# A transformer pair of blocks on one core: packed S5 near coefficients, swept first units, scores ahead of turned probabilities

## The chip, the cores and the metric

One core of a Trainium2 chip. The metric is device time in microseconds of one execution; a run's time is compared as the median of several runs.

## The reference

Two blocks of two layers each on a sequence of 256 tokens, width 1024, in fp32. What the change touches, cut down:

```python
def _mixer_s5(h, ...):                 # 64 groups of 16 channels, 64 complex states each, two directions
    bu = einsum('sgc,gpc->sgp', us, b_bar[direction])
    h  = associative_scan(a, bu, reverse=(direction == 1))
    y += einsum('sgp,gcp->sgc', h_re, c_re) - einsum('sgp,gcp->sgc', h_im, c_im)
    z  = gelu(y + d_skip * u);  return (z @ w_glu_a) * sigmoid(z @ w_glu_b)

x = x + gate_f * (square(relu(h @ w_fc1)) @ w_fc2)              # the MLP after each mixer of the first block

def swa_sink_attention(q, k, v, sinks):                          # window 128, 16 heads on 4 kv heads
    scores = where(valid, q @ k.T / 8, -inf);  m = maximum(max(scores), sink)
    e = exp(scores - m);  probs = e / (sum(e) + exp(sink - m));  return probs @ v

h = h + sigmoid(rms_norm(h) @ gate_w) * (p_i @ proj_w)           # per-layer embedding, in both layers
```

## The kernel before

**Layout.** Activations lie transposed, 8 tiles of 128 channels by 256 tokens (`xT`, `hT`, `sq`). Weights come as 1 MB blocks (8 tiles of 128 rows by 256 columns) into a ring of four, loaded by SP in the order of `weight_plan`; block b waits until block b-4 has been used (`blocks_done`). One block makes one unit: two output tiles in one PSUM bank.

**Split products.** In the phases of `SPLIT_LO` a weight and an activation are each split into a rounded high part and a low rest, and three fast products (high by high, high by low, low by high) replace one exact fp32 product. ACT rounds the weight block into one of two slots of `w_high` (`round_to`, L761), DVE subtracts (`lower_to`, L1895), PE multiplies (`block_products`, L1289, L1291, L1293). Activations go the same way after a norm: DVE makes `hT` = x times gain times rstd, ACT rounds it into `sq` (L768 or L770, `a_high`), DVE puts the rest back into `hT` (L1902, L2190 or L2328, `a_low`). The first unit after a norm (`split_arrived`) waits for `a_low` of tile k before its three products of k. Phases that begin so: `fc1_0`, `fc1_1`, `xbc`, `ple_gate_0`, `q`, `ple_gate_1`. Other phases use exact fp32 products (L1296).

**S5.** The sequence is cut into 32 chunks of 8 tokens. Coefficients are built during `fc1_0` and `fc2_0` in eight steps m of 8 groups: DVE products, PE transposes (L1487) and short products (`s5_kernels`, L1508, L1515), ACT copies and stores. What one chunk does to itself (the near part) is a kernel per group, `kext`, 16 channels by 240 columns, copied from PSUM by DVE (L2118, L2119) and stored by ACT (`store_kernels`, L915) into `k_dram`, from where `load_near` (L674) reads for each of four sets of 16 groups a Toeplitz arrangement, 128 partitions by 2048 floats, in eight DMAs. The sets go into the two slots of `w_high` in turn, so set 2 waits for unit 0 of `s5_out` and set 3 for unit 1. In `s5_in` PE makes chunk inputs (L1575), turns them (L1587), and adds turned parts (L1598); DVE scans (L2274, L2276) and turns back; ACT copies states (`copy_states`, L1011, L1012); `s5_out` has four units (L1640) of near products and of two far products with blocks `s5_far` (L695), two blocks a unit. gelu(n) (L1020) follows on ACT, `turn_z` (L1609) on PE, then `glu`, whose first block ACT may split into `w_high` only when the near sets there have been read.

The SP loop, where the order is written:

```python
if b >= RING:
    sp.wait_ge(blocks_done, b - RING + 1)
if b in NEAR_AT:
    load_near(NEAR_AT.index(b))
```

**Attention.** Eight tiles t of two heads. PE: `scores(t)` (L1806, L1807), `turn_probs(t)` (L1818), `attend(t)` (L1829 to L1831), with the gate's projection units at t = 0, 1, 3, 5. DVE: `masked(t)` (L2578, maxima L2584) and `normalised(t)` (L2598 to L2604); ACT: `exponents(t)` (L1212), `copy_turned(t)` (L1222), and the gate's silu (L1230) with a change of activation table before and after it. PE's order in an iteration is gate, `turn_probs(t)`, `scores(t+2)`, `attend(t-1)`; DVE's is `normalised(t)`, `masked(t+2)`, gated output of t-1. `probs` has two slots.

## Time and profile before

| | |
|---|---|
| median of 3 runs | 1275.17 us (1273.91 to 1281.21) |
| the profiled execution's own time | 1277.91 us |
| its span | 1276.1 us |
| PE busy | 1178.3 us (92%) |
| DVE busy | 790.1 us (62%) |
| ACT busy | 549.2 us (43%) |
| SP's queue, share of 16 DMA engines | 42.1% |

Times in the views are microseconds from the start of the span. Matmuls are pipelined, so a busy PE is not PE at its peak, and the distance between the starts of two matmuls tells more than their durations. A row of the timeline merges neighbouring instructions of one kind; its last bracket is the idle time ahead of the row and what ended it.

### The profile page before, as it was taken

To read this page: it belongs to the slowest core of one execution; us is meant where nothing else is said; L and a number is where in the kernel's file an instruction comes from. 1 tells how busy PE (TensorE), PEld (TensorE's weight loads), DVE (VectorE), ACT (ScalarE), POOL (GpSimd) and SP (SyncE) were. 2 spreads that over 40 slices of the span, in tenths; PEclk is the share of its full clock that TensorE was granted. 3 is DMA by queue.
4 is the path that set the end of the run, shared out by engine and by line. 5 is a ranking of instruction groups with operands and counts; after the bars stand their busy time and mean duration, and the time that the engine had idled before them with its cause. 6 is when DMAs were issued, how large, how long until landed. Compare 5 with 4: busy or idle time off the path is not lost.

```text
span 1276.1 us, 21870 instructions
## 1 busy us (share of the span) xinstructions
PE 1178.3 (92%) x9390; PEld 1043.0 (82%) x9390; DVE 790.1 (62%) x1342; ACT 549.2 (43%) x856; POOL 44.4 (3%) x71
## 2 busy tenths in 40 slices
PE   5999789999999998679999999999999999977798
PEld 2777567898888885479899999899888998866697
DVE  0188346876678765845666544598879635576535
ACT  1111224454111145444555434466667545476544
POOL 0100000000000000000000000000000000230000
PEclk8899989999999998979999999999899999999899
DMA  9976635899868945975355555134223443232041
GB/s 388 395 265 251 228 138 218 297 329 339 309 255 221 299 157 218 209 252 174 133 198 170 195 169 194 66 133 165 100 100 102 163 165 133 100 129 70 34 165 34
DMA packets 44448, 244.41 MB, mean 192 GB/s; under 512 B 4800, under 2 KB 15200, under 8 KB 15680
## 3 DMA queue, kind: packets, MB, share of 16 engines
q1 hardware_dynamic: 34272, 181.32, 42.1%
q0 software_dynamic: 6240, 43.94, 9.2%
q10 hardware_dynamic: 3840, 17.76, 3.5%
q8 instruction: 74, 1.21, 0.4%
q14 instruction: 22, 0.18, 0.0%
HBM read 224.19 MB, written 18.81 MB: 190 GB/s over the span
## 4 chain that ended last, share of the span: by engine, by line
PE 81%; DVE 8%; ACT 4%; DMA 4%; SPq 1%; issue 1%; ACTq 0%; DVEq 0%
PE ps L1296 17%; PE ps L1289 15%; PE ps L1291 14%; PE ps L1293 14%; PE ps L1346 3%; PE ps L1389 2%; DMA more<-in_ada_w 2%; PE ps L1317 2%; PE ps L1673 1%; PE ps L1773 1%; PE ps L1487 1%; DMA ring<-in_blocks 1%; DVE ring_rounded L1895 1%; PE ps L1686 1%; DVE hT L2374 1%
## 5 line engine op out<-in xcount | busy, mean ns | idle before, releaser
L1289 PE MATMUL ps<-sq_rounded,w_high_rounded 128*128 128x256 f32 x1216 | 355.0, 292 | 8.2 <-DVE hT_rounded L1902 2.4
L1293 PE MATMUL ps<-sq_rounded,ring_rounded 128*128 128x256 f32 x1216 | 347.1, 285 | 0.0
L1895 DVE TENSOR_TENSOR ring_rounded<-ring,w_high_rounded 128x1024 fp32r<-128x1024 f32 x208 | 247.1, 1229 | 108.3 <-ACT w_high_rounded L761 108.1
L1291 PE MATMUL ps<-hT_rounded,w_high_rounded 128*128 128x256 f32 x1088 | 310.4, 285 | 0.0
L761 ACT ACTIVATE w_high_rounded<-ring 128x1024 fp32r<-128x1024 f32 x208 | 208.0, 1049 | 118.6 <-PE ps L1293 97.6
L1289 PEld LDWEIGHTS ps<-sq_rounded,w_high_rounded 128*128 128x128 f32 x1216 | 236.8, 195 | 25.2 <-issue 16.0
L1293 PEld LDWEIGHTS ps<-sq_rounded,ring_rounded 128*128 128x128 f32 x1216 | 236.6, 195 | 0.0
L1291 PEld LDWEIGHTS ps<-hT_rounded,w_high_rounded 128*128 128x128 f32 x1088 | 211.6, 194 | 0.1
L1289 PE MATMUL ps<-more_rounded,w_high_rounded 128*128 128x256 f32 x448 | 127.4, 284 | 1.6 <-issue 1.4
L1293 PE MATMUL ps<-more_rounded,ring_rounded 128*128 128x256 f32 x448 | 126.8, 283 | 0.0
L1296 PE MATMUL ps<-big,ring 128*128 128x256 f32 x512 | 113.6, 381 | 0.0
L1291 PE MATMUL ps<-big_rounded,w_high_rounded 128*128 128x256 f32 x384 | 108.7, 283 | 0.0
L1296 PEld LDWEIGHTS ps<-big,ring 128*128 128x128 f32 x512 | 96.3, 190 | 14.4 <-issue 1.6
L1289 PEld LDWEIGHTS ps<-more_rounded,w_high_rounded 128*128 128x128 f32 x448 | 86.0, 192 | 2.2 <-issue 2.1
L1293 PEld LDWEIGHTS ps<-more_rounded,ring_rounded 128*128 128x128 f32 x448 | 86.0, 192 | 0.0
L1296 PE MATMUL ps<-hT,ring 128*128 128x256 f32 x320 | 73.9, 390 | 1.7 <-ACT hT L829 1.7
L1291 PEld LDWEIGHTS ps<-big_rounded,w_high_rounded 128*128 128x128 f32 x384 | 73.7, 192 | 0.1
L1296 PEld LDWEIGHTS ps<-hT,ring 128*128 128x128 f32 x320 | 61.5, 195 | 13.9 <-issue 4.7
L904 ACT ACTIVATE big<-ps 128x512 f32<-128x512 f32 x32 | 19.1, 596 | 101.9 <-PE ps L1293 101.9
L924 ACT ACTIVATE we_t<-ps 128x512 f32<-128x512 f32 x32 | 17.4, 596 | 89.2 <-PE ps L1487 89.2
L1291 PE MATMUL ps<-mixT_rounded,w_high_rounded 128*128 128x256 f32 x192 | 55.0, 286 | 0.0
L1973 DVE SCALAR_TENSOR_TENSOR big<-big,cols 128x256 f32<-128x256 f32 x120 | 47.7, 480 | 0.0
(374 smaller groups left out, 1637.3 us busy)
## 6 DMA issues: line engine op xcount, KB each, us to landing
ring<-in_blocks SPq DMA_DIRECT2D x140, 1024.0 KB, 4.9
ada_w<-in_ada_w POOLq DMA_DIRECT2D x27, 1024.0 KB, 7.3
ada_more<-in_ada_w POOLq DMA_DIRECT2D x13, 1024.0 KB, 7.6
we_dram<-we_t ACTq DMA_DIRECT2D x8, 1024.0 KB, 7.9
ca_dram<-more ACTq DMA_DIRECT2D x8, 1024.0 KB, 9.8
ring<-we_dram SPq DMA_DIRECT2D x8, 1024.0 KB, 4.9
ring<-ca_dram SPq DMA_DIRECT2D x8, 1024.0 KB, 10.3
big<-in_ada_w SPq DMA_DIRECT2D x4, 1024.0 KB, 10.3
```

The costliest lines, as they stand in the source:

```text
L761: nc.scalar.activation(w_high[:, c % 2, ks], ring[:, b % RING, ks], ACT.Copy)\
L904: nc.scalar.activation(hid[:, 2 * n:2 * n + 2], unit(phase, n), ACT.Relu).then_inc(hid_relu, 1)
L924: nc.scalar.activation(we_t[:, 2 * b:2 * b + 2].rearrange("p g r x -> p (g r x)"), MISC[b % 2][:, :], ACT.Copy).then_inc(we_copied, 1)
L1289: nc.tensor.matmul(out, high[:, k, columns], x_high, start=start, stop=False, skip_group_check=True)
L1291: nc.tensor.matmul(out, high[:, k, columns], x_low, start=False, stop=False, skip_group_check=True)
L1293: last = nc.tensor.matmul(out, low[:, k, columns], x_high, start=False, stop=stop, skip_group_check=True)
L1296: last = nc.tensor.matmul(out, w[:, k, columns], x, start=start, stop=stop, skip_group_check=True)
L1317: last = nc.tensor.matmul(ps[:, i], lhs[:, k, P * i:P * i + P], w[:, k], start=(k == 0), stop=(k == KB - 1))
L1346: last = nc.tensor.matmul(SPARE[j:j + COPIES, 0:NB], c_spread[:, k, PIECES - 1 - piece:PIECES - 1 - piece + COPIES], w[:, k], start=(piece ...
L1389: last = nc.tensor.matmul(STAT[:, 0:T], ones, squares(i)[:, k], start=(k == 0), stop=(k == DT - 1))
L1895: nc.vector.tensor_tensor(rounded(w), w, w_high[:, c % 2, ks], ALU.subtract)\
L1973: ins = nc.vector.scalar_tensor_tensor(out=conv[:, k], in0=apad[:, k, tap:tap + T], scalar=w, in1=conv[:, k], op0=ALU.mult, op1=ALU.add)
```

## The change

- `k_dram` becomes (4, 128, 240, 4): four steps of one partition's kernel side by side. `kext` gets a lane for each of two steps m by two groups; DVE writes a lane with a step of four elements, ACT stores once for two steps, all 128 partitions. `load_near` still makes eight DMAs a set, now of rows of 2 KB instead of 512 bytes. PE reads near[:, q, :, a], a step of four elements.
- Near sets 2 and 3 go to `big[2048:6144]` and are loaded ahead of far blocks 1 and 2; each set has a semaphore. glu's first two blocks wait for units 0 and 1 of `s5_out` only.
- `swept` does the first unit in three sweeps over both output tiles; DVE does all eight norms first and all eight lowerings then.
- `scores(t+2)` stands ahead of `turn_probs(t)`; `probs` has three slots and `att_high` moves behind it.

```diff
@@ -214,8 +214,8 @@
-    NEAR_AT = (first_block["fc2_0"] + 10, first_block["fc2_0"] + 11, first_block["s5_out"] + 1 + RING,
-               first_block["s5_out"] + 3 + RING)
+    NEAR_AT = (first_block["fc2_0"] + 10, first_block["fc2_0"] + 11, first_block["s5_out"] + 1,
+               first_block["s5_out"] + 2)
...
@@ -259,7 +259,7 @@
-        k_dram = nc.dram_tensor("k_dram", (GROUPS, GC, WIN), F32, kind="Internal").ap()
+        k_dram = nc.dram_tensor("k_dram", (GROUPS // 16, P, WIN, 4), F32, kind="Internal").ap()
...
@@ -303,7 +303,9 @@
-        s5_near = w_high_plain[:, :, :, :].rearrange("p s a b -> p s (a b)").rearrange("p s (g x) -> p s g x", x=P)
+        s5_near = [x.rearrange("p (q x) -> p q x", q=4)
+                   for x in (*(w_high_plain[:, n].rearrange("p a b -> p (a b)") for n in range(2)),
+                             big[:, 2048:4096], big[:, 4096:6144])]
...
@@ -498,7 +500,8 @@
-        kext, at = carve(more, at, 2, WIN)
+        kext, at = carve(more, at, WIN, 4)
+        assert at <= 8192
...
@@ -575,7 +578,8 @@
-        probs, at = carve(more, at, 2, 2, SEG)
+        probs, at = carve(more, at, 3, 2, SEG)
+        at_probs_end = at
...
@@ -584,7 +588,7 @@
-        att_high, _ = carve(more, 4096, ATT_TILES, T)
+        att_high, _ = carve(more, at_probs_end, ATT_TILES, T)
...
@@ -669,11 +673,13 @@
-                sp.wait_ge(k_stored, 64 * (2 * n + 2))
+                sp.wait_ge(k_stored, 16 * (n + 1))
+                if n == 2:
+                    sp.wait_ge(u_psum, 4)
-                    sp.dma_start(s5_near[GC * j:GC * j + GC, n % 2],
-                                 k_dram[16 * n:16 * n + 16, :, (L - 1 - j) * GC:(L - 1 - j) * GC + P]
-                                 .rearrange("g c x -> c g x")).then_inc(near_here[n % 2], 16)
+                    sp.dma_start(s5_near[n][GC * j:GC * j + GC],
+                                 k_dram[n].rearrange("(q c) x a -> c q (x a)", q=4)
+                                 [0:GC, :, 4 * (L - 1 - j) * GC:4 * (L - 1 - j) * GC + 4 * P]).then_inc(near_here[n], 16)
...
@@ -753,7 +759,7 @@
-                        act.wait_ge(blocks_done, first_block["glu"] - 2 * (1 - near_read))
+                        act.wait_ge(blocks_done, first_block["s5_out"] + 2 + 2 * near_read)
...
@@ -910,10 +916,9 @@
-                act.wait_ge(kext_ready, m + 1)
-                for q in range(4):
-                    act.dma_start(k_dram.rearrange("(a q) c x -> q c a x", q=4)[q, :, 2 * m:2 * m + 2, :],
-                                  kext[32 * q:32 * q + GC, :, :]).then_inc(k_stored, 16)
+                if m % 2:
+                    act.wait_ge(kext_ready, m + 1)
+                    act.dma_start(k_dram[m // 2], kext).then_inc(k_stored, 16)
...
@@ -1331,6 +1336,34 @@
+            def swept(phase, n, unit=None):
+                b = first_block[phase] + n
+                ps = pair(start_unit(phase, n if unit is None else unit))
+                high, low = w_high[:, split_place[b] % 2], rounded(ring[:, b % RING])
+                x_high, x_low = rounded(sq[:, :, :]), rounded(hT[:, :, :])
+                for k in range(KB):
+                    if k % 4 == 0:
+                        pe.wait_ge(w_high_ready, 2 * split_place[b] + k // 4 + 1)
+                    pe.wait_ge(a_high, SET_BASE[phase] + k + 1)
+                    for i in range(2):
+                        nc.tensor.matmul(ps[:, i], high[:, k, P * i:P * i + P], x_high[:, k], start=(k == 0 and i == 0),
+                                         stop=False, skip_group_check=True)
+                for k in range(KB):
+                    if k % 4 == 0:
+                        pe.wait_ge(w_low_vector, 2 * split_low[b] - 1 + k // 4)
+                    for i in range(2):
+                        nc.tensor.matmul(ps[:, i], low[:, k, P * i:P * i + P], x_high[:, k], start=False, stop=False,
+                                         skip_group_check=True)
+                for k in range(KB):
+                    pe.wait_ge(a_low, SET_BASE[phase] + k + 1)
+                    for i in range(2):
+                        last = nc.tensor.matmul(ps[:, i], high[:, k, P * i:P * i + P], x_low[:, k], start=False,
+                                                stop=(k == KB - 1), skip_group_check=True)
+                last.then_inc(blocks_done, 1)
...
@@ -1517,7 +1550,10 @@
-                project("fc1_0", n, (sq, hT), split_arrived("fc1_0") if n == 0 else None)
+                if n == 0:
+                    swept("fc1_0", 0)
+                else:
+                    project("fc1_0", n, (sq, hT))
...
@@ -1634,7 +1670,7 @@
-                                lhs, rhs = u_in[:, 16 * n + g], near[:, g]
+                                lhs, rhs = u_in[:, 16 * n + g], near[:, q, :, a]
...
@@ -1847,9 +1894,9 @@
-                turn_probs(t)
+                turn_probs(t)
...
@@ -2110,16 +2157,18 @@
-                if m > 0:
-                    dve.wait_ge(k_stored, 64 * m)
-                else:
+                if m == 0:
+                elif m % 2 == 0:
+                    dve.wait_ge(k_stored, 16 * (m // 2))
-                nc.vector.tensor_copy(kext[:, :, 0:edge], STAT[:, 0:2 * P].rearrange("p (a x) -> p a x", a=2)[:, :, 0:edge])
-                link(nc.vector.tensor_copy(kext[:, :, edge:WIN], MISC[2][:, 0:2 * P].rearrange("p (a x) -> p a x", a=2)))
+                lane = 2 * (m % 2)
+                out = kext[:, :, lane:lane + 2].rearrange("p x a -> p a x")
+                nc.vector.tensor_copy(out[:, :, 0:edge], STAT[:, 0:2 * P].rearrange("p (a x) -> p a x", a=2)[:, :, 0:edge])
+                link(nc.vector.tensor_copy(out[:, :, edge:WIN], MISC[2][:, 0:2 * P].rearrange("p (a x) -> p a x", a=2)))
-                    mid = kext[:, a, edge:P]
+                    mid = kext[:, edge:P, lane + a]
...
@@ -2369,12 +2414,11 @@
-                for k in range(DT + 2):
-                    if k < DT:
-                        nc.vector.scalar_tensor_tensor(out=hT[:, k], in0=xT[:, k], scalar=col(name, first + k),
-                                                       in1=rstd[:, :], op0=ALU.mult, op1=ALU.mult).then_inc(hn_ready, 1)
-                    if k >= 2:
-                        lower_tiles(phase, k - 2, hT[:, k - 2], sq[:, k - 2])
+                for k in range(DT):
+                    nc.vector.scalar_tensor_tensor(out=hT[:, k], in0=xT[:, k], scalar=col(name, first + k),
+                                                   in1=rstd[:, :], op0=ALU.mult, op1=ALU.mult).then_inc(hn_ready, 1)
+                for k in range(DT):
+                    lower_tiles(phase, k, hT[:, k], sq[:, k])
...
@@ -2572,16 +2616,16 @@
-                if t >= 2:
-                    dve.wait_ge(pt_psum, 2 * (t - 1))
+                if t >= 3:
+                    dve.wait_ge(pt_psum, 2 * (t - 2))
-                    ins = nc.vector.scalar_tensor_tensor(out=probs[:, t % 2, h], in0=MISC[h][:, 0:SEG], scalar=64 ** -0.5,
+                    ins = nc.vector.scalar_tensor_tensor(out=probs[:, t % 3, h], in0=MISC[h][:, 0:SEG], scalar=64 ** -0.5,
-                        ins = nc.vector.tensor_reduce(row_max[:, t, 2 * h + b:2 * h + b + 1], probs[:, t % 2, h, lo:hi],
+                        ins = nc.vector.tensor_reduce(row_max[:, t, 2 * h + b:2 * h + b + 1], probs[:, t % 3, h, lo:hi],
```

The call of `swept` stands in the same way in `fc1_1`, `xbc`, both `ple_gate` phases and `q`; DVE's loops in `fc1_0` and `fc1_1` are split like the one in `split_norm`.

## Rows read from the trace of the kernel before

**Rows 1.** Chain that ended last, whole span: share by engine.

```profile
PE 81%; DVE 8%; ACT 4%; DMA 4%; SPq 1%; issue 1%; ACTq 0%; DVEq 0%
```

**Rows 2.** Timeline, first unit of `fc1_0`: start, length, engine, line, idle before.

```profile
209.00 1.28 DVE L2185 SCALAR_TENSOR_TENSOR hT<-xT,gains,rstd 128x256 f32<-128x256 f32 x3 [3.78 <-ACT rstd L815]
209.52 1.31 ACT L770 ACTIVATE sq_rounded<-hT,mods 128x256 fp32r<-128x256 f32 x3 [0.55 <-DVE hT L2185]
...
214.16 1.27 DVE L2190 SCALAR_TENSOR_TENSOR hT_rounded<-hT,mods,sq_rounded 128x256 fp32r<-128x256 f32 x3
...
218.57 0.28 PE L1291 MATMUL ps<-hT_rounded,w_high_rounded 128*128 128x256 f32 x1
218.69 0.28 PE L1293 MATMUL ps<-sq_rounded,ring_rounded 128*128 128x256 f32 x1
```

**Rows 3.** Timeline, `ple_gate_0`: first norm, and ACT reading the first unit.

```profile
1050.37 1.28 DVE L2374 SCALAR_TENSOR_TENSOR hT<-xT,cols,rstd 128x256 f32<-128x256 f32 x3 [8.36 <-ACT rstd L815]
...
1059.95 0.60 ACT L1168 ACTIVATE ada_w<-ps 128x512 f32<-128x512 f32 x1 [0.99 <-PE ps L1293]
```

**Rows 4.** ACT queue, first store; waits, 203 to 475: total, times, longest.

```profile
302.78 4.80 ACTq L915 DMA_DIRECT2D k_dram<-more  x4
...
PE ps L1289 <- DVE ring_rounded L1895: 1.4, 1, 1.4
```

**Rows 5.** Timeline of DVE: last residual of `fc2_0`, a plain and a stepped copy.

```profile
470.99 0.88 DVE L1946 SCALAR_TENSOR_TENSOR xT<-ps,mods,xT 128x256 f32<-128x256 f32 x2 [0.91 <-PE ps L1296]
...
484.59 0.69 DVE L2244 COPY hT<-ps 128x512 f32<-128x512 f32 x1
...
538.08 1.99 DVE L2299 COPY mixT<-ps 128x512 f32<-128x512 f32 x2
```

**Rows 6.** Timeline, `s5_out` and the start of `glu`.

```profile
514.65 0.43 PE L1640 MATMUL ps<-w_high,hT 128*32 128x128 f32 x8 [1.68 <-ACT ada_more L1012]
...
527.93 9.41 SPq L674 DMA_DIRECT2D w_high<-k_dram  x8
...
533.85 0.43 PE L1640 MATMUL ps<-w_high,hT 128*32 128x128 f32 x8
...
539.96 0.61 ACT L1012 ACTIVATE ada_more<-we_t 64x496 f32<-64x496 f32 x1
...
547.26 0.66 PE L1640 MATMUL ps<-w_high,hT 128*32 128x128 f32 x8 [10.58 <-DMA w_high<-k_dram]
...
551.94 2.00 ACT L761 ACTIVATE w_high_rounded<-ring 128x1024 fp32r<-128x1024 f32 x2 [10.74 <-DMA ring<-in_blocks]
...
554.89 0.57 ACT L1020 ACTIVATE big<-ps 128x512 f32<-128x512 f32 x1
...
557.14 0.56 PE L1289 MATMUL ps<-sq_rounded,w_high_rounded 128*128 128x256 f32 x1
```

**Rows 7.** Stretches: length, granted clock, share of 16 DMA engines, GB/s.

```profile
512.00:514.00 2.00, 1.00 0.88 373
...
524.00:526.00 2.00, 0.50 1.26 117
```

**Rows 8.** L1640 in unit 1: length, PE, PEld, granted clock, DMA share, GB/s.

```profile
523.50:527.90 4.40, 4.34 (x96) 4.09 (x96) 0.64 1.25 114
```

**Rows 9.** DVE's waits, 1135 to 1232: total, times, longest.

```profile
DVE more L2578 <- PE ps L1807: 16.2, 6, 4.7
```

**Rows 10.** Timeline, attention: scores(2), gate(2), turn 4, gate(3), turn 7.

```profile
1151.10 1.07 PE L1807 MATMUL ps<-big 64*128 64x256 f32 x4
...
1175.42 0.60 ACT L1230 ACTIVATE more<-ps 128x512 f32<-128x512 f32 x1 [3.84 <-PE ps L1293]
...
1181.33 0.91 PE L1818 MATMUL ps<-const,more 128*128 128x128 f32 x6 [3.35 <-DVE more L2604]
...
1191.67 0.60 ACT L1230 ACTIVATE more<-ps 128x512 f32<-128x512 f32 x1 [5.24 <-PE ps L1293]
...
1202.65 1.54 PE L1818 MATMUL ps<-const,more 128*128 128x128 f32 x6 [2.18 <-DVE more L2604]
```

More of the change, by code:

```diff
@@ L378, in program @@
         k_stored = sem("k_stored")
-        near_here = [sem(f"near_here{i}") for i in range(2)]
+        near_here = [sem(f"near_here{i}") for i in range(4)]
         rot_args = sem("rot_args")
@@ L1211, in exponents @@
                         i = 2 * h + b
-                        nc.scalar.activation(probs[:, t % 2, h, lo:hi], probs[:, t % 2, h, lo:hi], ACT.Exp,
+                        nc.scalar.activation(probs[:, t % 3, h, lo:hi], probs[:, t % 3, h, lo:hi], ACT.Exp,
                                              bias=neg_max[:, t, i:i + 1], scale=1.0,
@@ L1648, in _ @@
             for n in range(16):
-                project("fc1_1", n, (sq, hT), split_arrived("fc1_1") if n == 0 else None)
+                if n == 0:
+                    swept("fc1_1", 0)
+                else:
+                    project("fc1_1", n, (sq, hT))
             for n in range(4):
@@ L1701, in _ @@
             for m in range(XBC_UNITS):
-                project("xbc", m, (sq, hT), split_arrived("xbc") if m == 0 else None)
+                if m == 0:
+                    swept("xbc", 0)
+                else:
+                    project("xbc", m, (sq, hT))
                 if m == 0:
@@ L1777, in embedding @@
                 for n in range(4):
-                    project(f"ple_gate_{layer}", n, (sq, hT),
-                            split_arrived(f"ple_gate_{layer}") if n == 0 else None)
+                    if n == 0:
+                        swept(f"ple_gate_{layer}", 0)
+                    else:
+                        project(f"ple_gate_{layer}", n, (sq, hT))
             embedding(0, 6)
@@ L1837, in _ @@
             for n in range(4):
-                project("q", n, (sq, hT), split_arrived("q") if n == 0 else None)
+                if n == 0:
+                    swept("q", 0)
+                else:
+                    project("q", n, (sq, hT))
                 head_stats(n + 1)
@@ L2320, in _ @@
             dve.wait_ge(rstd_ready, 4)
[L2321 to L2329 removed]
+            for k in range(DT):
+                nc.vector.scalar_tensor_tensor(out=hT[:, k], in0=xT[:, k], scalar=gains[:, 3, k:k + 1],
+                                               in1=rstd[:, :], op0=ALU.mult, op1=ALU.mult).then_inc(hn_ready, 1)
+            for k in range(DT):
+                dve.wait_ge(a_high, SET_BASE["fc1_1"] + k + 1)
+                nc.vector.scalar_tensor_tensor(out=rounded(hT[:, k]), in0=hT[:, k], scalar=mod(1, SHIFT_F, k),
+                                               in1=rounded(sq[:, k]), op0=ALU.add, op1=ALU.subtract).then_inc(a_low, 1)
             def square_unit(base, n):
@@ L2602, in normalised @@
                         i = 2 * h + b
-                        a = probs[:, t % 2, h, lo:hi]
+                        a = probs[:, t % 3, h, lo:hi]
                         ins = nc.vector.tensor_scalar(a, a, row_inv[:, t, i:i + 1], None, ALU.mult)
```

34 lines of the change are left out of this document (12 added, 22 removed).

## The prediction

> **What bounds the kernel now.** I read the chain that ended last first [rows 1]: PE carries 81% of it, DVE 8%, ACT 4%, DMA 4%. So the matmuls set the time nearly everywhere, and an edit pays only where PE stands still or is paced by another engine. I then took the waits of PE and DVE, and for each place where the diff touches the order of work the timeline around it. Four such places matter: the first unit after a norm, the ACT queue during `fc1_0`, the end of `s5_out`, and the loop over attention tiles.
>
> **1. First units in sweeps (`swept`).** Before, a first unit does its first output half (i=0) k by k, high times `x_high`, high times `x_low`, low times `x_high`, and each k waits for DVE's lowering of that k; only then comes the second half. In `fc1_0` DVE's first norm starts at 209.00, DVE alternates norm and lowering, its last lowering ends at 214.16+1.27 = 215.43, and the unit's last matmul ends at 218.69+0.28 = 218.97 [rows 2]: 10.0 us after the first norm. Matmuls follow each other at 218.69−218.57 = 0.12 us when nothing holds them.
>
> After: eight norms back to back (three take 1.28, so one each 0.40), ACT's rounding follows 0.52 behind (209.52 against 209.00) and ends 0.52 + 7×0.40 + 0.5 = 3.8 after the first norm. Sweep one ends two matmuls and a hand-off later, at about 4.25. Sweeps two and three are 32 matmuls, 3.84: end at 8.1. Sweep three starts at 6.2 and needs its last lowered tile at about 7.8; DVE does the same sixteen operations as before and is done at 6.4, so it hides. Gain 10.0−8.1 = 1.9, and the same in `fc1_1`, whose timeline repeats this one. In `xbc` and the two `ple_gate` phases the unit takes 1059.95−1050.37 = 9.6 [rows 3]; the rounding there has no bias and ends 0.1 sooner, so the end is 8.0 and the gain 1.6. In `q` it is nothing: its norms and lowerings lie under PE's `kv` units, and if that cover were gone it would be 1.6 more. Sum 2×1.9 + 3×1.6 = 8.6. From below: sweep one could gain nothing if hand-offs grew; from above, 10.0 less 16 matmuls' work hidden, about 2.9 each.
>
> **2. Packed coefficients, the store.** 32 stores on ACT's queue become 4. The first four hold ACT for 4.80 us, and only after them comes the split of the next weight block; PE waits 1.4 for its low part [rows 4]. The change issues no store for m=0, so that wait goes: 1.4. The other 28 issues lie under PE's `fc2_0` matmuls, where PE waits for no store, so I cost them at nothing, gain too. DVE now writes `kext` with a step of four elements. The nearest rows are DVE's copies of 128x512: stepped into `mixT` 1.99 for two, plain into `hT` 0.69 for one [rows 5], so a kernel's two copies, half as long each, may cost 0.3 to 0.4 more. Under `fc2_0` that hides; for the last, m=7, DVE reaches the next residual 0.91 ahead of PE [rows 5], which covers it. Without that cover it is 0.4.
>
> **3. Near sets 2 and 3 early.** Before, SP issues near set 3 only when `s5_out` unit 2 is under way: eight DMAs from 527.93, 9.41 us of SP's time, with far block 7 and the first glu blocks queued behind. ACT has the last states at 539.96+0.61 = 540.6, but unit 3 starts at 547.26, 10.58 of it on that load. The glu block then lands at 551.9, its split runs, gelu(3) follows at 554.89, and glu's first matmul is at 557.14 [rows 6].
>
> After, both sets are asked for at far blocks 1 and 2, when `s5_in` blocks 5 and 6 are done, so unit 3 starts when its states are there, 540.7: 6.5 earlier. SP is free when unit 2, which starts at 533.85 [rows 6], is half done, about 535, so glu's block is in by about 540; ACT splits it behind gelu(2), 541.2 to 543.2, and rounds z until 544.4. Unit 3 at the slow clock takes 4.3 [rows 8] and ends at 545.0, gelu(3) 0.6, and glu starts 554.89−557.14, that is 2.25, after gelu(3)'s start: 547.3. Gain 557.1−547.3 = 9.8. What is late next is the chain DVE scan, ACT `copy_states(3)`, unit 3, and that is untouched.
>
> What the moved loads are moved past: far blocks 1, 2 and 3. A block of 1 MB moves at 373/0.88 = 424 GB/s, 2.5 us; a near set of 512-byte rows moves at 117 GB/s, 9.0 us [rows 7]. Packets are 8 KB and 512 B, so one takes an engine 309 ns and 70 ns; a straight line through the two gives 118 ns for the new 2 KB rows, 32 of them per engine, 3.8 us a set (an estimate; bounds 2.5 and 9.0). The queue is full until about 513.8 already, and its last two blocks are far 2 and far 3. So far 1 ends at 508.8+3.8 = 512.6, where unit 0, which starts at 514.65, wants it at its second half, 515.8; far 2 ends at 518.9 for unit 1's start at 523.5, far 3 at 521.4 for its second half at 525.7 [rows 6, 8]. Nothing stalls as long as a set takes less than about 6 us.
>
> PE reads a near set with a step of four elements. No row shows PE doing that. Unit 1 and unit 3 are exposed (behind unit 1 comes `add_turns(3)`, the last scan and unit 3); units 0 and 2 end before anybody waits. The near third of a unit of 4.34 is 1.4 us [rows 8]. Bounds: nothing, and doubled, 1.4 per unit; the nearest row, DVE's stepped copy, is 1.45 times the plain one, which at a slow PE clock I take as 0.5 per unit: −1.0. Beside it stands a rule of the Trainium skill (SBUF — State Buffer, section on Door 1: The DMA port swizzle): a stream that goes to a new 16-byte line with every element pays a penalty, and a step of four fp32 elements is just that. The DVE rows agree with it; taken as a doubling, the sum would be 1.8 us worse. Part 3 in all: 9.8−1.0 = 8.8.
>
> **4. Scores ahead, a third `probs` slot.** Before, `scores(t+2)` stands behind `turn_probs(t)`, which waits for DVE's `normalised(t)`, so DVE stands between `normalised(t)` and `masked(t+2)`: 16.2 us in six waits [rows 9]. After, `masked(t+2)` follows `normalised(t)` at once. Stepping through with the old durations: before gate(1), `turn_probs(0)` and `scores(2)` ended at 1152.2; now `scores(2)` is done in PE's idle time and gate(1) starts 1.6 earlier (of which 1.07 is the slow last part of scores [rows 10]). From the end of gate(2) to that of gate(3) it took 1191.67−1175.42 = 16.25, two serial loops: the gate's silu, table load, exponents, normalise, turn (1181.33, 5.9 after the gate [rows 10]), then masked scores, maxima, exponents, normalise, turn once more. After, the second tile's exponents no longer wait for the first one's turn: gate 5.8 (48 matmuls), 5.9 to the turn, 1.3 for turn and `attend`: 13.1. Gain 3.1, and the same for the period before. From gate(3) to the last turn 1202.65−1191.67 = 11.0 becomes 9.8: 1.2. Together 9.0; hand-offs I left out cost about 0.8: 8.2. Bounds 4 (one loop saved in two) and 9.0. ACT's silu and table loads are what bounds it next.
>
> **Sum.** 8.6 + 1.4 + 8.8 + 8.2 = 27.0. Against the profiled execution's own 1277.9 that is 1250.9. That execution lies 2.7 above the median of the runs, 1275.2; on the median the forecast is 1248.2.
>
> **Rivals.**
> *Far blocks late.* If 2 KB rows are no faster than 512-byte ones, a set takes 9.0: far 1 at 517.8 is 2.0 late, far 3 at 531.8 is 6.1 late, with landing some 7, and unit 1, the last scan and unit 3 slip by it. Most of part 3 goes: 1255. For it: the queue is full there. Against: the time per packet did depend on bytes.
> *Stepped reads dear.* If each near matmul took four times as long, units 1 and 3 lose 4.3 each: 1248.2+8.6−1.0 = 1256. For it DVE's stepped copy, against it the slow clock in both units. The Trainium skill's rule on 16-byte lines (same page and section) points this way.
> *Attention gives little.* If ACT's table loads or the slow clock bound each loop, 4 instead of 8.2, and with sweeps at half, 1257.
> *Slower.* The clock falls in the first sweep, whose matmuls come in pairs with gaps, and stays low. A matmul then costs about 0.21, and a unit of 48 takes 4.5 more. It takes 27.0 + 6.4 = 33.4, seven and a half slow units, one and a half after each of five sweeps, to end at 1282. Against: in the old first unit, with more gaps, matmuls still run 0.12 apart [rows 2].
> *No effect.* The near wait is replaced one for one (glu's block or far 7 is the true bound) and attention is ACT's: only sweeps and the store, 10 us, 1265.
>
> **Chances.** Forecast (1243 to 1253) 0.58; far late 0.12; reads dear 0.07; little from attention 0.11; no effect 0.05, of which 0.03 falls within half a per cent of before; slower 0.03; more than forecast (under 1243) 0.04. The range takes in forecast and the first three rivals, 1243 to 1258. Half a per cent, 6.4 us, is about what a measurement of this kernel can tell from no change: faster by more 0.94, within 0.03, slower 0.03.
>
> **What would show it.** In the profile after: first units ending 8 us after the first norm, with three runs of one matmul line each; no wait of PE for `big<-k_dram` and none for the low part near 308; near sets moving well over 200 GB/s; `s5_out` unit 3 starting within 0.2 us of ACT's last state copy, and glu's first matmul about 6.5 later; DVE's waits for L1807 nearly gone and gate ends 13 apart. Wrong if PE waits for `ring<-ca_dram`, if the stepped near matmuls come more than 0.1 us apart at full clock, or if the granted clock drops in a first unit.

## The result, and the profile after

The changed kernel takes 1255.8 us (median of 4 runs, 1254.93 to 1259.79), the kernel before, beside it, 1274.54 (4 runs): ratio 0.9847, 95% interval 0.9819 to 0.9874. Measured again beside eleven runs of the kernel before, it took 1252.47 (6 runs, 1243.36 to 1258.32) against 1277.65: 0.9799, 0.9754 to 0.9845. The forecast, 1248.2 on 1275.2, is a ratio of 0.979. So it is faster, inside the range, and by 19 to 25 us where 27.0 were forecast.

The profiled execution took 1255.34, its span is 1253.5 against 1276.1, at a mean granted clock of 0.969 against 0.962. The chain that ended last:

```profile
PE 85%; DMA 5%; ACT 4%; DVE 4%; issue 1%; SPq 1%; DVEq 0%
```

DVE's share has halved against [rows 1], DMA's has grown. Where DMA came in is the story of this case.

**The first unit of `fc1_0`**, in the timeline (start, length, engine, line, tiles, idle before):

```profile
209.30 3.26 DVE L2233 SCALAR_TENSOR_TENSOR hT<-xT,gains,rstd 128x256 f32<-128x256 f32 x8 [3.78 <-ACT rstd L821]
209.82 3.31 ACT L776 ACTIVATE sq_rounded<-hT,mods 128x256 fp32r<-128x256 f32 x8 [0.55 <-DVE hT L2233]
210.47 3.21 PE L1352 MATMUL ps<-sq_rounded,w_high_rounded 128*128 128x256 f32 x16
212.48 3.24 DVE L2237 SCALAR_TENSOR_TENSOR hT_rounded<-hT,mods,sq_rounded 128x256 fp32r<-128x256 f32 x8
213.52 2.08 PE L1358 MATMUL ps<-sq_rounded,ring_rounded 128*128 128x256 f32 x16
215.44 2.08 PE L1363 MATMUL ps<-hT_rounded,w_high_rounded 128*128 128x256 f32 x16
```

Three sweeps of one line each, the last one starting 6.14 after the first norm; the next unit's work (PE L1379) starts at 217.44, 8.14 after that norm. The forecast was 8.1, and 10.0 before [rows 2].

**The ACT queue during `fc1_0`**:

```profile
301.31 0.63 ACT L915 ACTIVATE big<-big 128x512 f32<-128x512 f32 x1 [0.40 <-ACT we_t L929]
301.84 1.99 ACT L767 ACTIVATE w_high_rounded<-ring 128x1024 fp32r<-128x1024 f32 x2
```

The 4.80 us of stores of [rows 4] are gone, the weight split follows at once, and PE waits for nothing between 290 and 320.

**`s5_out`.** First the waits of PE from 480 to 556 (total, times, longest), then the timeline:

```profile
PE ps L1676 <- DMA ring<-ca_dram: 5.3, 2, 4.9
```

```profile
497.78 4.35 SPq L680 DMA_DIRECT2D big<-k_dram  x8
502.18 0.43 SPq L701 DMA_DIRECT2D ring<-ca_dram  x1
502.81 3.58 SPq L680 DMA_DIRECT2D big<-k_dram  x8
...
517.87 0.66 PE L1676 MATMUL ps<-w_high,hT 128*32 128x128 f32 x8 [4.86 <-DMA ring<-ca_dram]
...
524.34 1.22 DVE L2321 TENSOR_TENSOR_SCAN more<-ada_more,ps 128x512 f32<-128x512 f32 x1 [4.69 <-PE ps L1634]
...
540.81 0.61 ACT L1017 ACTIVATE ada_more<-we_t 64x496 f32<-64x496 f32 x1
...
541.67 0.66 PE L1676 MATMUL ps<-big,hT 128*32 128x128 f32 x8 [2.90 <-ACT ada_more L1017]
...
546.34 0.60 ACT L1025 ACTIVATE big<-ps 128x512 f32<-128x512 f32 x1 [1.22 <-PE ps L1676]
...
547.83 0.36 PE L1294 MATMUL ps<-sq_rounded,w_high_rounded 128*128 128x256 f32 x1
```

The wait for the near set (10.58 in [rows 6]) is gone, and unit 3 starts 0.25 behind the end of ACT's last state copy. But that copy itself is late. Count from the end of `fc2_0`'s last residual (471.87 before, 468.99 now): the copy ended 68.7 after it and now ends 72.4 after it. So glu's first matmul (the last line above), 6.2 behind unit 3's start, comes 78.8 after the residual where it came 85.3: 6.4 gained where 8.8 were forecast. The reader can walk back: SP asks for both sets from 497.8 to 506.4, and for far block 1 between them. Unit 0's second half waits 4.86 for far 1 and starts at 517.87. Behind it on PE stands `add_turns(2)`, for which DVE's scan waits 4.69, and one scan later come the copies. The DMA traffic in two of the stretches between (length; busy time of PE, its weight loads, DVE, ACT and POOL; clock, DMA share, GB/s):

```profile
504.00:506.00 2.00, 1.68 (x17) 1.11 (x10) 1.93 (x4) 1.97 (x4) 0.00 (x0) 1.00 1.04 135
506.00:508.00 2.00, 2.00 (x6) 0.87 (x5) 1.93 (x4) 1.46 (x3) 0.00 (x0) 1.00 1.08 153
```

At 135 to 153 GB/s a set of 1.05 MB takes 7 to 8 us in this execution, not the 3.8 that I estimated; 117 GB/s it was with rows of 512 bytes [rows 7]. So the forecast's rival *Far blocks late* named the chain that holds this stage. Its 517.8 for far 1 is no hit, though: the residual now ends 2.9 earlier, so on the rival's clock far 1 came at 520.7, and the rival had the long wait at far 3 (6.1, here 0.4) and the short one at far 1 (2.0, here 4.9).

One slow set ahead of far 1 isn't the whole of it. The prediction counted two blocks back from the end of the queue's traffic and had far 1 in at 508.8. In the trace of the kernel before, far 1 is asked for at 501.4 and lands 9.6 later, at 511.0. On this kernel's clock, which runs 2.9 ahead, that is 508.1, and 7.3 for a set make 515.4. Far 1, asked for at 502.2 here, landed 15.6 later, at 517.8: 2.4 are still missing. The eight stretches of 2 us from 502 to 518 read 268, 135, 153, 199, 310, 245, 151 and 182 GB/s, which is 3.3 MB. Set 2 and far 1 are 2.1 of it. The rest is what was left of far 0 and a large part of set 3, though set 3 was asked for behind far 1; I take the 2.4 to be set 3's, which no run tried alone.

**Attention**, waits of PE and DVE, and the timeline of gates 2 and 3:

```profile
PE ps L1862 <- DVE more L2648: 12.2, 5, 3.5
...
DVE more L2622 <- PE ps L1851: 9.3, 3, 4.8
```

```profile
1156.76 0.60 ACT L1235 ACTIVATE more<-ps 128x512 f32<-128x512 f32 x1 [4.11 <-PE ps L1298]
...
1171.61 0.60 ACT L1235 ACTIVATE more<-ps 128x512 f32<-128x512 f32 x1 [3.83 <-PE ps L1298]
```

DVE waits 9.3 in three waits where it waited 16.2 in six [rows 9], and the gates' silus are 14.85 apart instead of 16.25 [rows 10].

**By stage.** Stages are cut at DVE's first norm of each phase (and at the end of `fc2_0`'s last residual). In us:

| stage | before | before, again | changed | changed, again | sweeps alone | attention alone | s5 alone | sets at far 3, 5 |
|---|---|---|---|---|---|---|---|---|
| `fc1_0` norm to last residual | 262.87 | 263.42 | 259.69 | 259.70 | 261.00 | 263.66 | 262.31 | 259.70 |
| to `fc1_1` norm (holds s5) | 137.95 | 134.53 | 131.17 | 129.73 | 136.96 | 134.60 | 130.49 | 126.46 |
| to `xbc` norm | 201.70 | 201.70 | 199.94 | 199.94 | 199.92 | 201.70 | 202.44 | 199.93 |
| to `ple_gate_0` norm | 238.85 | 238.73 | 237.52 | 235.93 | 237.64 | 239.10 | 233.08 | 235.25 |
| to `q` norm | 36.06 | 36.05 | 35.10 | 34.60 | 34.62 | 36.32 | 36.04 | 34.61 |
| to `ple_gate_1` norm (attention) | 156.73 | 159.23 | 149.31 | 145.54 | 157.69 | 147.10 | 158.15 | 149.29 |
| to the end | 32.94 | 32.94 | 31.47 | 31.46 | 31.49 | 32.92 | 32.92 | 31.48 |

Where PE runs without waits, stages repeat to 0.1, with s5 alone's 202.44 as the one exception. The s5 stage, the one before `ple_gate_0` and attention differ by 1 to 4 us between two executions of the same code, so no single pair of profiles gives their gain. The clearest case is the 233.08 of s5 alone before `ple_gate_0`, 5.7 under the kernel before in a stage that its part doesn't touch: from 900 to 950 its granted clock is 1.00, that of the kernel before 0.90.

### The profile page after: what moved, and what is told of

Same layout as the page of the kernel before. It is cut to its first block, busy times and chain, and to the rows that moved or that the text cites. A ratio compares the mean times of both kernels' runs of the same rounds, so it can differ in the third digit from the quotient of the medians.

```text
span 1253.5 us, 21837 instructions
## 1 busy us (share of the span) xinstructions
PE 1176.6 (94%) x9390; PEld 1041.6 (83%) x9390; DVE 792.5 (63%) x1342; ACT 547.5 (44%) x856; POOL 44.6 (4%) x71
## 4 chain that ended last, share of the span: by engine, by line
PE 85%; DMA 5%; ACT 4%; DVE 4%; issue 1%; SPq 1%; DVEq 0%
PE ps L1301 18%; PE ps L1294 15%; PE ps L1296 14%; PE ps L1298 14%; PE ps L1379 3%; PE ps L1422 2%; PE ps L1322 2%; DMA ring<-ca_dram 2%; PE ps L1712 1%; DMA ring<-in_blocks 1%; PE ps L1352 1%; DMA more<-in_ada_w 1%; PE ps L1412 1%; PE ps L1815 1%; PE ps L1520 1%
## 5 line engine op out<-in xcount | busy, mean ns | idle before, releaser
L1294 PE MATMUL ps<-sq_rounded,w_high_rounded 128*128 128x256 f32 x1120 | 324.0, 289 | 1.7 <-DVE mixT_rounded L1949 1.3
L1298 PE MATMUL ps<-sq_rounded,ring_rounded 128*128 128x256 f32 x1120 | 319.4, 285 | 0.0
L1296 PE MATMUL ps<-hT_rounded,w_high_rounded 128*128 128x256 f32 x992 | 283.5, 286 | 0.0
L1294 PEld LDWEIGHTS ps<-sq_rounded,w_high_rounded 128*128 128x128 f32 x1120 | 217.8, 194 | 11.1 <-issue 8.1
L1298 PEld LDWEIGHTS ps<-sq_rounded,ring_rounded 128*128 128x128 f32 x1120 | 217.7, 194 | 0.0
L1296 PEld LDWEIGHTS ps<-hT_rounded,w_high_rounded 128*128 128x128 f32 x992 | 193.4, 195 | 0.1
```

Source lines behind the costliest of these rows:

```text
L1294: nc.tensor.matmul(out, high[:, k, columns], x_high, start=start, stop=False, skip_group_check=True)
L1296: nc.tensor.matmul(out, high[:, k, columns], x_low, start=False, stop=False, skip_group_check=True)
L1298: last = nc.tensor.matmul(out, low[:, k, columns], x_high, start=False, stop=stop, skip_group_check=True)
```

## The experiments

### The two kernels once more

No edit.

> The changed kernel once more, to narrow its ratio, since the two profiled executions differ by 22.6 us and the medians by 18.7. If the gain of the profiles is the true one: 0.982 of the kernel before. If that of the medians: 0.985. The stage anchors of the profile should repeat within 0.5 us: fc1_0's first norm 209.3, fc1_1's 600.2, xbc's 800.1, the last tile's 1248.8.

> The kernel before once more, for the size of what differs between two executions of one kernel. If the 2.7 us by which the first profiled execution lay above the median are a lower clock in the stages where PE is waited for, s5 and attention differ by 1 to 4 us between the two executions, and the stages where PE runs without waits (fc1_1's norm to xbc's: 201.7) by under 0.2.

The changed kernel: ratio 0.9799 (0.9754 to 0.9845), profiled at a span of 1246.3 and clock 0.972, 7.2 less than the first. The table shows where: 1.4 in s5, 1.6 before `ple_gate_0`, 3.8 in attention; its unit 0 waited 2.7 for far 1 instead of 4.9. The anchors of `fc1_1` and `xbc`, 598.8 and 798.8, missed what I expected by 1.3; of the two expected ratios the interval holds 0.982 and just leaves out 0.985. While set 2 moves:

```profile
504.00:506.00 2.00, 1.68 (x14) 1.12 (x11) 1.96 (x3) 1.96 (x4) 0.00 (x0) 1.00 1.06 189
506.00:508.00 2.00, 2.00 (x6) 0.94 (x5) 1.94 (x3) 1.28 (x3) 0.00 (x0) 1.00 1.17 236
```

The same code, the same DMAs and the same stretches as above, at 189 and 236 GB/s instead of 135 and 153: a set took about 5 us here. Far 1, asked for at 502.10, landed at 515.5, which by the same count is 2.3 later than one set of this length explains. The granted clock from 1130 to 1170 was 0.88 and 0.86 in the first execution, 1.00 and 0.99 in the second. The kernel before took 1277.99, and its s5 stage 3.4 less than in the first profile, its attention 2.5 more. The wait for the near set was 8.6 instead of 10.6:

```profile
PE ps L1640 <- DMA w_high<-k_dram: 8.6, 1, 8.6
```

### Each part alone

The kernel before with one part of the change and nothing else; the edits are the diff's own, cut along its parts.

```diff
 # sweeps alone
+                if n == 0:
+                    swept("fc1_0", 0)
...
+            for k in range(DT):    # all norms, then all lowerings
 # attention alone
+                if t + 2 < ATT_TILES:
+                    scores(t + 2)
                 turn_probs(t)
-                if t + 2 < ATT_TILES:
-                    scores(t + 2)
 # s5 alone: kext, k_dram and s5_near packed, NEAR_AT at far 1 and 2
```

> The kernel before with the sweeps alone (swept first units, DVE's norms ahead of its lowerings). The prediction's sum: 8.6 us less, 0.9933 of the kernel before. From the two profiles, stage by stage, 1.9 + 1.8 + 1.3 + 1.0 + 1.5 = 7.5 us, 0.9941. Rival, that the sweeps give half because what they save is waited for again at the next unit (its split weights, DVE's lowering of the next block): 4 us, 0.997.

> The kernel before with the attention part alone (scores(t+2) ahead of turn_probs(t), a third probs slot). The prediction's sum: 8.2 us less, 0.9936. If ACT's table loads and the lower clock bound each loop: 4 us, 0.997. The waits of DVE for the scores' matmuls should fall from 16.2 to about 9 us, those of PE for normalised from 18 to 12.

> The kernel before with the packed coefficients and the early near sets alone. The prediction's sum: 1.4 + 8.8 = 10.2 us less, 0.9920. From the profiles, with the far blocks late: 1.3 + 6.8 = 8.1 us or, if unit 0 waits less for far 1 as in the second execution, 9.5: 0.993. PE should again wait 3 to 5 us for the far blocks in unit 0 or 1.

Measured, against 17 runs of the kernel before (1278.04): sweeps 1266.51, ratio 0.9918 (0.9897 to 0.9940), which is 10.5 us; attention 1265.95, 0.9911 (0.9888 to 0.9933), 11.4 us; s5 1269.52, 0.9940 (0.9917 to 0.9963), 7.7 us. The three sum to 29.6, each with some 3 us either way, which agrees with the 25.7 of the second measurement of the whole. In attention alone DVE waits 6.6 for the scores' matmuls (9 expected) and PE 12.4 for `normalised` (12 expected). All rivals that gave a part half its gain fall for the sweeps and for attention. In s5 alone PE's wait for the far blocks is there as well:

```profile
PE ps L1672 <- DMA ring<-ca_dram: 3.8, 1, 3.8
```

### The same loads, later

```diff
-               first_block["s5_out"] + 1, first_block["s5_out"] + 2)
+               first_block["s5_out"] + 4, first_block["s5_out"] + 6)    # second run: + 3, + 5
```

> The changed kernel with near sets 2 and 3 asked for at far blocks 4 and 6 instead of 1 and 2; all else is kept, the packed layout, the stepped reads and the tiles of their own too. Theory A (the two sets, 7 us each, stand before far 1 and far 2, so that unit 0's second half comes 4.9 late and with it the last two scans): PE's waits for ring<-ca_dram at 512:518 go, DVE's scan after them starts near 519.7 instead of 524.3, the last state copy ends 4 to 6 us earlier than 541.4, and the time falls by 3 to 5 us, to about 1251.5; set 3 then stands before far 6 and 7, so that a wait of up to 2 us for them is possible in unit 3. Theory B (the stepped reads of PE are what kept the gain small): units take as long as now, the time stays within 1 us of the changed kernel's, 1255.8.

> As the run before, but the sets at far blocks 3 and 5, one place earlier each: far 3 is needed only at unit 1's second half, near 521, and far 5 at unit 2's second half, which nothing waits for. Theory A: the same 3 to 5 us for the scans, and no wait in unit 3, since far 6 and 7 are in by 536 and the next glu block by 539: 1250.5. Theory B: 1255.8.

Sets at far 3 and 5: 1249.72, ratio 0.9784 (0.9749 to 0.9818). PE doesn't wait for any far block, and the timeline of PE reads

```profile
512.95 0.65 PE L1676 MATMUL ps<-w_high,hT 128*32 128x128 f32 x8
...
536.79 0.65 PE L1676 MATMUL ps<-big,hT 128*32 128x128 f32 x8 [2.64 <-ACT ada_more L1017]
```

Unit 0 runs through and unit 3 starts at 536.79 instead of 541.67 and 539.53 in the two executions of the changed kernel, whose stages up to there take the same 259.7. The stage falls to 126.46, 4.7 and 3.3 less. Theory A holds in this stage, with its size; the runs of the whole kernel (1249.72 beside 1252.47) are too close together to show it.

Sets at far 4 and 6: 1253.7, 0.9813 (0.9780 to 0.9846). Unit 0 is free here too, but far 6 and 7 now stand behind set 3:

```profile
PE ps L1676 <- DMA ring<-ca_dram: 4.3, 1, 4.3
```

I had allowed 2 us for it and expected 1251.5. The stage takes 131.74, as in the changed kernel: one late block traded for another.

### The stepped reads

```diff
-                near = s5_near[n].rearrange("p q (x a) -> p q x a", a=4)
+                near = s5_near[n]
...
-                                lhs, rhs = u_in[:, 16 * n + g], near[:, q, :, a]
+                                lhs, rhs = u_in[:, 16 * n + g], near[:, q, P * a:P * a + P]
```

> The changed kernel with each near matmul reading 128 adjacent elements instead of every fourth one (the coefficients that it then multiplies are in the wrong order, so the output isn't the reference's; counts and sizes are the same). Theory A: unit 0 is late anyway, so only units 1 and 3 count; eight near matmuls take 0.22 instead of 0.44 us at full clock and the same 0.45 at the lower one, so unit 1 and unit 2 fall from 3.8 to 2.9 and unit 3 from 4.6 to 4.1: the time falls by 0.5 to 1.3 us, to about 1254.9. Theory B (reads are the main loss): by 3 us or more.

This kernel multiplies by the near coefficients in a wrong order, with the counts and sizes of the changed one. 1253.16, 0.9807 (0.9773 to 0.9841), not to be told from the changed kernel. Its unit 3 ran at full clock (1.00 from 541 to 546) and the changed kernel's mostly at half (0.66), so the stages don't compare, but the eight matmuls do. The timeline of PE in unit 0 shows eight near matmuls and the far ones that follow; the difference of the starts is what the eight take. First this kernel at full clock, then the changed kernel at full and at half clock:

```profile
511.24 0.43 PE L1676 MATMUL ps<-w_high,hT 128*32 128x128 f32 x8 [1.71 <-ACT ada_more L1017]
511.45 0.65 PE L1676 MATMUL ps<-ring,ada_more 128*32 128x128 f32 x16
```

```profile
511.02 0.65 PE L1676 MATMUL ps<-w_high,hT 128*32 128x128 f32 x8 [1.68 <-ACT ada_more L1017]
511.46 0.65 PE L1676 MATMUL ps<-ring,ada_more 128*32 128x128 f32 x16
...
519.16 0.67 PE L1676 MATMUL ps<-w_high,hT 128*32 128x128 f32 x8
519.62 1.05 PE L1676 MATMUL ps<-ring,ada_more 128*32 128x128 f32 x16
```

0.21 for eight plain ones, 0.44 for eight stepped ones at full clock, 0.46 at half clock, where the plain ones take 0.40 to 0.43 (unit 1 before is such a stretch [rows 8]). So the step doubles the price at full clock, 0.9 a unit, and costs 0.03 to 0.06 per eight, 0.1 to 0.2 a unit, at half.

### Rows of 512 bytes again

```diff
-        k_dram = nc.dram_tensor("k_dram", (GROUPS // 16, P, WIN, 4), F32, kind="Internal").ap()
+        k_dram = nc.dram_tensor("k_dram", (GROUPS, GC, WIN), F32, kind="Internal").ap()
...
-                                lhs, rhs = u_in[:, 16 * n + g], near[:, q, :, a]
+                                lhs, rhs = u_in[:, 16 * n + g], near[:, g]
```

> The changed kernel with the old layout of the coefficients (32 stores, rows of 512 bytes, PE's near reads of adjacent elements), the two sets still asked for at far 1 and 2 into tiles of their own. If row size matters by what the two traces show, 9.0 against 7.2 us a set, unit 0's second half and unit 1 wait 2 to 3.5 us longer for the far blocks; ACT's stores at 302 hold PE 1.4 again, and the plain reads give 0.5 back: 3 to 4 us more than the changed kernel, 1256. If it doesn't matter (16 partitions a DMA do): 1 us more, 1253.5.

1257.78, 0.9842 (0.9822 to 0.9861), about 5 us over the changed kernel's second measurement and 2 over its first. Its stages say 2.0 more up to the last residual and 2.3 to 3.8 more in s5. While a set moves:

```profile
508.00:510.00 2.00, 1.68 (x10) 1.06 (x9) 1.93 (x4) 1.94 (x5) 0.00 (x0) 1.00 1.21 133
510.00:512.00 2.00, 2.00 (x6) 0.95 (x5) 1.93 (x4) 1.22 (x3) 0.00 (x0) 1.00 1.23 154
```

That is the rate of the packed kernel in its first execution (135 and 153) and well under that in its second (189 and 236). So rows four times as long raised the rate of a set by something between nothing and a half, where my straight line had 2.4 times. PE waits 7.8 for far blocks, 2.5 and 3.6 more than in the two executions of the changed kernel, and the time is beyond the 1256 that I expected if row size matters, not at the 1253.5 of the other case. This kernel's SP also needs 5.75 and 6.59 us to issue the two sets, against 4.35 and 3.58, and far 2 is asked for 44.8 us after the last residual instead of 37.5. Whether the slower rows or the later asking makes the 2 to 4 us more in s5, no run tried.

### What holds a set back

First, four DMAs over 128 partitions instead of eight over 16, with the shifted windows kept (PE reads the blocks of a kernel backwards).

```diff
-                for j in range(L):
-                    sp.dma_start(s5_near[n][GC * j:GC * j + GC], ...
+                for q in range(4):
+                    sp.dma_start(s5_near[n][:, q],
+                                 bass.AP(tensor=first.tensor, offset=first.offset,
+                                         ap=[[4 * GC, L], [4 * WIN, GC], [1, 4 * P]])).then_inc(near_here[n], 16)
```

> The changed kernel, its sets asked for at the same places, each by four DMAs that write all 128 partitions (32 to 34 of 2 KB rows for an engine, as now) instead of eight that write 16 partitions each; for that the blocks of a kernel stand in reverse order in DRAM and PE reads them backwards. Theory C (a DMA into 16 partitions is what holds a set to 140 GB/s): a set moves at over 300 GB/s, in 3 us instead of 7; unit 0's and unit 1's waits for the far blocks go (4.2 to 5.3 us in the two executions), the last state copy ends at 536 to 537 instead of 539.3 and 541.4, and the time is that of the sets at far 3 and 5 or a little less, 1249. Theory D (rows of 2 KB are what holds it): 7 us a set and 1252.5 as now.

1257.67, 0.9836 (0.9814 to 0.9858), and PE waits 10.1 for far blocks. Neither theory said this. SP issued the first set in less time (2.49), but everything moved at about half of the block rate for over 20 us:

```profile
506.00:508.00 2.00, 1.68 (x19) 1.07 (x10) 1.93 (x4) 1.95 (x5) 0.00 (x0) 1.00 1.04 217
...
522.00:524.00 2.00, 2.00 (x15) 0.90 (x8) 0.00 (x0) 1.65 (x2) 0.00 (x0) 0.63 1.01 208
```

The outermost dimension of this source is 8. Of that the Trainium skill (DMA: Bandwidth & Descriptors, section Why a DMA increments its semaphore by 16 and not by 1) says that a DMA is put on as many engines, up to 16, as divide the slowest dimension of both sides, here 8 of 16. That alone doesn't explain the rate. With eight engines idle the DMA share would read near 0.5, and it reads 1.04 and 1.01: the engines as a whole were busy twice as long for each byte, for the blocks as well. No view here shows which engines worked. A source that one DMA reads in eight overlapping windows is the other thing that is new here, and no run separates the two. The next run takes both away: the same bytes and rows of 2 KB, without the shift inside a DMA, so the outermost dimension is 128; the near coefficients that it multiplies by are others.

```diff
+                for q in range(4):
+                    sp.dma_start(s5_near[n][:, q],
+                                 k_dram[n].rearrange("p x a -> p (x a)")[:, 64 * q:64 * q + 512])\
+                        .then_inc(near_here[n], 16)
```

> All four near sets loaded by four DMAs each from the stored coefficients row by row, 128 partitions and rows of 2 KB, without the shifted windows (so the near coefficients are others than the reference's and the output is wrong in that part; bytes and row length of a set are those of the changed kernel). The run with 128 partitions and shifted windows moved both its sets and the blocks behind them at 215 GB/s, half the block rate; its outermost source dimension is 8. Theory C (what counts is how a DMA spreads over partitions and engines): here the outermost dimension is 128, a set moves at 350 GB/s or more, in 3 us, and unit 0's and unit 1's waits for the far blocks go; the last state copy ends 67 to 68 after fc2_0's last residual instead of 70.2 and 72.4; 1249. Theory D (2 KB rows are slow by themselves): 140 to 220 GB/s again, waits of 4 us or more, 1253 to 1257.

```profile
506.00:508.00 2.00, 1.68 (x21) 1.03 (x14) 1.93 (x4) 1.95 (x5) 0.00 (x0) 1.00 1.07 412
508.00:510.00 2.00, 2.00 (x6) 0.89 (x6) 1.93 (x4) 1.65 (x3) 0.00 (x0) 1.00 1.05 429
```

A set moves at the rate of a weight block, 1.05 MB in 2.5 us, with the sets still ahead of far 1 and 2. No wait for a far block; the s5 stage is 126.75, that of the sets at far 3 and 5; 1250.18, 0.9761 (0.9732 to 0.9790). The last state copy ends 67.7 after the residual, as expected (67 to 68). So neither the place in the queue nor rows of 2 KB cost anything by themselves: what costs is how a set's DMAs are cut. What this run leaves open is which part of the cut, since two things went together. A DMA of the changed kernel writes 16 partitions, and its eight DMAs read each of 64 stored rows in eight windows, 64 floats apart; here a DMA writes 128, and four DMAs read each of 128 rows in four such windows. Overlap between DMAs is therefore still there, at half the count, and costs nothing, which speaks for the partitions. So does the Trainium skill (SBUF — State Buffer, section Door 1: The DMA port swizzle): partitions 0 to 15 reach four of 16 ports, measured there at 104 GB/s. The 117 to 154 of three executions here lie near that and not at the block rate, but the 189 and 236 of the changed kernel's second one are about twice it, so eight such DMAs behind one another aren't held to that figure. And the run before this one, with 128 partitions, was no faster than that execution. The partitions are the likely cause and not the shown one.

Last, the sets on POOL's queue, beside SP's.

```diff
+            for n in (2, 3):
+                pool.wait_ge(blocks_done, first_block["s5_out"] + n - RING)
+                load_near(n, pool)
             pool.wait_ge(blocks_done, first_block["glu"])
```

> The changed kernel with near sets 2 and 3 issued from POOL's queue instead of SP's, at the same block counts, the same sixteen-partition DMAs; POOL is idle there. If a set is slow because few partitions take its bytes, other engines' and ports' time is free beside it, so that far 1 to 3 run at the same time: both sets and three blocks, 5 MB, in 12 to 16 us from 502 instead of 22, no wait for far blocks in unit 0, the last state copy at 536.5, 1249 to 1250. If the 16 DMA engines are what is busy (their share was 1.04 to 1.13 while a set moved), the blocks slow down by what the sets take, unit 0 waits 2 to 5 us as now, and the time stays at 1252.5.

```profile
516.00:518.00 2.00, 2.00 (x15) 0.89 (x6) 1.93 (x4) 0.99 (x2) 0.00 (x0) 1.00 1.09 268
526.00:528.00 2.00, 2.00 (x44) 1.68 (x36) 0.34 (x1) 1.60 (x3) 0.00 (x0) 0.50 1.00 250
```

The two queues share 215 to 268 GB/s for 30 us, and PE waits 5.4 for far blocks, in units 0, 1 and 2: the second of the two cases that I had expected. A slow DMA keeps the engines busy for the blocks beside it as well. The s5 stage is 130.64, no better; 1252.12, 0.9779 (0.9748 to 0.9810).

## Why the prediction was right, and where it missed

**Sweeps, 8.6.** Right. The stages give 2.3 (`fc1_0`: 263.3 in the mean of three kernels without sweeps or the new store, 261.00 with sweeps alone), 1.78 in `fc1_1`, 1.2 or more in `xbc`, whose stage is noisy, 1.44 in `ple_gate_0` and 1.47 in `ple_gate_1`: 8.2. For `q` I had forecast nothing, and the stage that holds it shows nothing: 157.69 with sweeps alone, between the 156.73 and 159.23 of the kernel before. The lower clock in a first sweep (*Slower*) never came: the granted clock is 1.00 in the 8 us of each of these five units, in both executions.

**Store, 1.4.** Right: 261.00 with sweeps alone, 259.7 with the store as well, 1.3; 1.0 in s5 alone. The stepped `kext` copies cost 0.38 more for each m (0.557 and 0.624 against 0.389 and 0.415), as forecast, and hid.

**s5, 8.8.** This step failed, and in the sentence that a 2 KB set takes 3.8 us. It was a straight line through two kinds of packets, and it took row length for the cause. But the two rows differed also in how many partitions a DMA reaches: a block's goes to 128, a near set's to 16. A set with long rows still took 7 to 8 in one execution and about 5 in the other. A second sentence failed with it, that nothing stalls under about 6 us a set: at 5 us far 1 still came 2.7 late. It started from far 1 in at 508.8, where the trace of the kernel before has 511.0, and it gave set 3, asked for right behind far 1, no effect; 2.4 and 2.3 us remain open in the two executions, with set 3 the likely cause. The chain itself, a slow set, then far 1, unit 0, the scans and the last copy, the prediction had named, as a rival. Stage by stage: 136.0 in the mean of the four executions with the old near loads (134.5 to 138.0), 130.5 in the mean of the three with the new ones (both executions of the changed kernel, and s5 alone), 5.5 gained. With the far blocks freed, 126.5 with the sets later and 126.75 with fast sets at the old place: 9.3 to 9.5. So all else in part 3 was sized rightly (8.8), and about 4 were lost to this, which one or two executions each can't give closer than to 1 or 2 us. In the first pair of profiles the two executions hid some of it: there the stage fell by 6.8.

**Stepped reads, −1.0.** The mechanism was right and the size depends on the clock: 0.9 a unit at full clock, up to 0.2 at half. The Trainium skill's rule on 16-byte lines (SBUF — State Buffer, section Door 1: The DMA port swizzle) is borne out at full clock, where the price doubles (0.21 to 0.44). Of the two exposed units, unit 1 ran at full clock and unit 3 mostly at half in the changed kernel: 0.9 and up to 0.2, which is the 1.0 of the forecast with another split. *Stepped reads dear* is out.

**Attention, 8.2.** Under-sized. 157.9 in the mean of the four executions without the part (156.7 to 159.2), 148.2 in the mean of the ten with it (145.5 to 150.3): 9.8, above the upper bound of 9.0. At full clock the gates come as I stepped them: 13.57 and 13.29 apart in the second execution, against the 13.1 of the forecast. Where the 1.6 beyond it come from, the parts of the loop that I did not step through or the lower clock that falls on each kernel differently in this stage, stays open. *Attention gives little* and *No effect* are out.

**The sum.** By stages 8.2 + 1.3 + 5.5 + 9.8 = 24.8 against 27.0: s5 gave 3.3 less and attention 1.6 more. The second measurement says 25.7 and the first one 19.5 (0.0153 of 1274.5, interval 16 to 23); the first had only four runs of each kernel, and executions of the changed kernel reach from 1243.36 to 1259.79. The two profiles shown differ by 22.6, with the kernel before in its dearer s5 stage and the changed one in its dearer attention. That the time fell inside the range says little: the range took in three rivals, up to 1258. The first measurement, 1255.8, is outside the 1243 to 1253 of the forecast itself and beside the 1255 of *Far blocks late*; the second, 1252.47, is just inside. That attention gave back half of what s5 lost is luck.

**The best version** is the changed kernel with the sets at far 3 and 5: 1249.72, beside 1252.47 for the changed kernel in the same comparison. The runs alone don't separate the two (intervals 0.9749 to 0.9818 and 0.9754 to 0.9845); the s5 stage does, by 3.3 to 4.7.

## What to carry to other kernels

Before a load is moved ahead of others, take its rate from a row of a DMA of the same shape, in partitions written, order of the source and row length alike: a line drawn through rows that differ in two of these gives the price to the wrong one. Take it from two executions. A slow transfer in a full queue costs the blocks behind it at least its own length, on another queue as well; look for the place where the block behind it is needed last, and try one place on either side, since far 3 and 5 gained 3 to 5 us of the stage where far 1 and 2 and far 4 and 6 did not. Cut the trace into stages and take two executions of each kernel before a difference of 4 us in one stage is explained.

## What the runs showed of the hardware that I had not expected

- A set of 1.05 MB by DMAs into 16 partitions moved at 133 to 154 GB/s with rows of 512 bytes, and with rows of 2 KB at 135 to 153 in one execution and 189 to 236 in the next; by DMAs over 128 partitions with an outermost source dimension of 128 it went at the blocks' own rate (412 to 429), and with one of 8, read in overlapping windows, at 208 to 217, with the weight blocks behind it held to that rate too.
- A block of 1 MB asked for between two such sets landed 15.6 us later in one execution and 13.4 in the next; 2.4 and 2.3 of that are neither its time in the queue before nor the set ahead of it.
- Two queues with one slow stream in them ran at 215 to 268 GB/s together, at a DMA share of 1.0: a busy share says nothing of bytes.
- PE's matmuls of 128 columns with a moving operand of every fourth fp32 element: 0.44 us for eight against 0.21 at full clock, 0.46 against 0.40 to 0.43 at half.
- The granted clock's dips fall differently in two executions of one kernel (0.969 and 0.972 in the mean; from 1130 to 1170 0.88 and 0.86 against 1.00 and 0.99), and the spans differ by 7.2 us.
